# Attention of a hybrid layer: another order of rows, queries loaded by row, keys and values by separate semaphores

## The reference

```python
z = jnp.einsum('bthd,bshd->bhts', qb, kb)
strict = jnp.arange(t1)[None, :] < jnp.arange(t0, t1)[:, None]
log_beta = jax.nn.log_sigmoid(z)
log_keep = jnp.where(strict, jax.nn.log_sigmoid(-z), 0.0)
after = lax.cumsum(log_keep, axis=3, reverse=True) - log_keep
A = jnp.where(strict, jnp.exp(log_beta + after), 0.0)
outs.append(jnp.einsum('bhts,bshd->bthd', A, vb))
```

## Time and profile before

| | us |
|---|---|
| runs of the kernel, median of 3 (lowest, highest) | 3392.56 (3388.01, 3393.36) |
| the profiled execution: its own time | 3387.77 |
| the profiled execution: its span | 3386.0 |
| TensorE busy in it, matmuls | 3247.3 |
| VectorE busy in it | 2425.2 |
| ScalarE busy in it | 1926.0 |
| GpSimd busy in it | 884.7 |

### The profile page before, as it was taken

One profiled execution on the slowest core, in us unless ns is written; L12 is line 12 of the kernel. 1 busy time (PEld: TensorE's weight loads), 2 busy tenths in 40 slices (PEclk: granted clock), 3 DMA queues, 4 the chain that ended last, 5 costly groups with the idle time before them and its releaser, 6 DMA issues. The chain is left out here.

```text
span 3386.0 us, 72847 instructions
## 1 busy us (share of the span) xinstructions
PE 3247.3 (96%) x28402; PEld 2678.1 (79%) x28402; DVE 2425.2 (72%) x2989; ACT 1926.0 (57%) x4177; POOL 884.7 (26%) x677
## 2 busy tenths in 40 slices
PE   6998999999999999997999999999999998999998
PEld 4786888999999997886777677767767776888887
DVE  4765345434568894234999999989999997666665
ACT  4553112222334452224898888888889897555554
POOL 1323333200000003431223422523262325232322
PEclk8999999999999999998999999999999999999999
DMA  8889878877955578985001201120111013666664
GB/s 296 327 323 319 270 256 297 308 238 237 311 177 189 184 241 304 322 280 177 21 28 56 76 28 32 59 70 26 46 58 53 12 38 95 183 212 190 206 201 135
DMA packets 415600, 582.65 MB, mean 172 GB/s; under 512 B 35568, under 2 KB 298096, under 8 KB 414288
## 3 DMA queue, kind: packets, MB, share of 16 engines
q1 hardware_dynamic: 394560, 506.56, 45.5%
q0 software_dynamic: 16960, 58.73, 5.1%
q10 hardware_dynamic: 3792, 13.30, 1.0%
HBM read 393.74 MB, written 184.75 MB: 171 GB/s over the span
## 5 line engine op out<-in xcount | busy, mean ns | idle before, releaser
L1492 DVE TENSOR_TENSOR_SCAN a_ring<-a_ring,a_zeros 128x1024 f32<-128x1024 f32 (+6 forms) x640 | 1237.1, 2009 | 31.5 <-ACT a_ring L1417 25.6
L1431 ACT COPY a_turned<-a_rt 128x512 f32<-128x512 f32 x960 | 529.8, 622 | 113.2 <-PE a_rt L1339 112.8
L1417 ACT ACTIVATE a_ring<-a_z 128x512 f32<-128x512 f32 (+3 forms) x1152 | 561.4, 595 | 17.0 <-PE a_z L1323 16.9
L1352 PE MATMUL a_acc<-a_turned,c_dw 128*64 128x256 f32 x4352 | 524.5, 382 | 4.8 <-ACT a_osum L1441 4.8
L1339 PEld LDWEIGHTS a_rt<-c_ident,a_ring 64*128 64x128 f32 x8448 | 330.2, 138 | 179.9 <-issue 103.2
L1339 PE MATMUL a_rt<-c_ident,a_ring 64*128 64x64 f32 x8448 | 369.5, 226 | 46.4 <-ACT a_turned L1431 22.6
L1299 POOL TENSOR_SCALAR_AFFINE_SELECT a_ring<-a_ring 128x256 f32<-128x256 f32 x128 | 198.8, 1568 | 820.9 <-ACT a_ring L1417 820.9
L1352 PEld LDWEIGHTS a_acc<-a_turned,c_dw 128*64 128x64 f32 x4352 | 289.2, 137 | 152.2 <-ACT a_turned L1429 8.8
L1323 PE MATMUL a_z<-c_khi,a_q 64*128 64x512 f32 (+3 forms) x2304 | 373.2, 400 | 26.6 <-DMA c_dw<-scratch_dw 12.6
L939 DVE TENSOR_TENSOR p_hlo<-p_wraw,p_hlo 128x1024 fp32r<-128x1024 f32 x85 | 104.4, 1228 | 324.3 <-ACT p_hlo L704 324.3
L704 ACT CAST p_hlo<-p_wraw 128x1024 fp32r<-128x1024 f32 x85 | 89.1, 1048 | 392.4 <-PE p_bank L572 210.8
(11 more groups left out here) (298 smaller groups left out, 6418.9 us busy)
## 6 DMA issues: line engine op xcount, KB each, us to landing
p_hlo<-scratch_parts SPq DMA_DIRECT2D x130, 512.0 KB, 5.0
p_wraw<-scratch_sums SPq DMA_DIRECT2D x128, 512.0 KB, 6.6
p_aslot<-scratch_parts SPq DMA_DIRECT2D x62, 512.0 KB, 5.0
p_u<-in_w_in POOLq DMA_DIRECT2D x64, 256.0 KB, 5.4
scratch_wsums<-p_u POOLq DMA_DIRECT2D x32, 512.0 KB, 6.4
p_hraw<-scratch_sbv POOLq DMA_DIRECT2D x32, 512.0 KB, 7.3
m_xt<-in_x SPq DMA_DIRECT2D x32, 512.0 KB, 5.2
out_y<-c_pair SPq DMA_DIRECT2D x32, 512.0 KB, 4.5
```

Source lines behind the costliest of these rows:

```text
L1352: last = pe.matmul(acc[h * SD:(h + 1) * SD, lo:QW], dw[:, h, j * TPC + kb, :], turned[:, (FIRST[u] + kb // 2) % TB, kb % 2, h * QW + lo:(h ...
L1417: act.activation(ring[:, slot, s, part, 0:w], z[at % ZB][:, 0:w], ACT.Sigmoid, scale=-Z_SCALE).then_inc(keep_done, 1)
L1431: act.copy(dst, src).then_inc(turned_done, 1)
L1492: return dve.tensor_tensor_scan(line, line, zeros[:, 0:1].to_broadcast([P, right - left]), first, ALU.mult, ALU.add)
```

## The change

The rows of a pair of heads are taken in another order, written as a list: 15, 14, 13, 0, 12, 1, 11, 10, ... 2. The two rows of one unit so stand behind the two rows of seven units, and the last rows of a pair of heads have 2 and 2 units. Queries are loaded by row (256 columns) into four buffers; those of row r + 4 are issued when the scores of row r are all done. Keys and values of a chunk get separate semaphores: TensorE waits for the keys at the scores and for the values at the weighing. For the next heads the keys of a chunk are loaded when the scores of the last row that uses it are done, and its values behind that row's store. Row r - 1 is stored after the loads of row r. The two constants for the mixing stage move behind the last loop. Ten semaphores are passed on from the projection stage with the values that they have reached there (V_BEFORE, Q_BEFORE). The diff, cut to its core:

```diff
+    ORDER = [15, 14, 13, 0, 12, 1] + list(range(11, 1, -1))
+    FREE_AT = {}
+    for chunk in range(NCH - 1, -1, -1):
+        FREE_AT.setdefault(max(ORDER.index(2 * chunk), ORDER.index(2 * chunk + 1)) if chunk else NR - 1, []).append(chunk)
...
-        q_sb = sb("q", [P, 2, 2, CH], F32R)
+        QB = 4
+        q_sb = sb("q", [P, QB, 2, QW], F32R)
...
-        chunk_in = [sem(f"chunk_in{k}") for k in range(NCH)]
-        q_in = [sem("q_in0"), sem("q_in1")]
+        chunk_in, value_in = [sem(f"chunk_in{k}") for k in range(NCH)], loads[:NCH]
+        q_in = [sem("q_in0"), sem("q_in1"), loads[KT], loads[KT + 1]]
+        Q_BEFORE, V_BEFORE = (0, 0, 16 * NCH, 16), 32
...
                 load_keys(0, k)
+                load_values(0, k)
                 if k == NCH - 1:
-                    load_queries(sp, 1)
+                    for row in range(1, QB):
+                        load_queries(sp, row)
...
-            for g in range(NP * NCH):
-                hp, c, row = g // NCH, NCH - 1 - g % NCH, 2 * g
-                if g + 2 < NP * NCH:
-                    sp.wait_ge(z_done, 4 * (LAST[row + 1] + 1))
-                    load_queries(sp, g + 2)
...
-                store(row)
...
-                store(row + 1)
-                if hp + 1 < NP:
-                    load_keys(hp + 1, c)
-                elif c == 2:
-                    sp.wait_ge(m_out, 16)
-                    for chunk in range(2):
-                        load_mix(sp, d, mix_in, chunk, chunk, held["ch_in"])
+            def finish_row(row):
+                hp, at = row // NR, row % NR
+                store(row)
+                if hp + 1 < NP:
+                    for chunk in FREE_AT.get(at, ()):
+                        load_values(hp + 1, chunk)
+                elif at == NR - 3:
+                    sp.wait_ge(m_out, 16)
+                    for chunk in range(2):
+                        load_mix(sp, d, mix_in, chunk, chunk, held["ch_in"])
+
+            for row in range(NP * NR):
+                hp, at = row // NR, row % NR
+                sp.wait_ge(z_done, 4 * (LAST[row] + 1))
+                if row + QB < NP * NR:
+                    load_queries(sp, row + QB)
+                if hp + 1 < NP:
+                    for chunk in FREE_AT.get(at, ()):
+                        load_keys(hp + 1, chunk)
...
+                if row:
+                    finish_row(row - 1)
...
+            finish_row(NP * NR - 1)
...
-                pe.wait_ge(chunk_in[j], 64 * (hp + 1))
+                pe.wait_ge(chunk_in[j], 32 * (hp + 1))
...
             def weigh(u):
-                _, row, cb, j = UNITS[u]
+                hp, row, cb, j = UNITS[u]
+                pe.wait_ge(value_in[j], V_BEFORE + 32 * (hp + 1))
```

## The result

| | before | changed kernel |
|---|---|---|
| median of the runs, us (lowest to highest) | 3391.88 (3388.01 to 3393.36, 4 runs) | 3373.34 (3369.12 to 3377.02, 4 runs) |
| the profiled execution's own time | 3387.77 | 3377.02 |
| its span | 3386.0 | 3375.2 |

The ratio is 0.995, with a 95% interval of 0.9937 to 0.9962. The change makes the kernel 18.5 us faster on the medians; 3370 had been forecast, in a range of 3362 to 3386. The profiled execution of the changed kernel is the slowest of its four.

The account below looks back on a forecast made before the run. The vector engine's scan was taken to bound attention, so only its gaps and the end could be won. −17.06 − 5.85 + 2.1 − 2 = −22.8 us on the median 3392.56 gave 3370, range 3362 to 3386.

Parts of the forecast that it names:

- handover gaps: Scan's three gaps between pairs of heads, 5.06, 6.97 and 5.03 us, would all go with earlier queries: −17.06 us.
- mask waits: Scan of the last one-unit row waits 1.46 us for its mask, four times; the new order removes this: −5.85 us.
- gaps behind short pairs: Behind short pairs of scans the next pair waits for ScalarE's sigmoid: 7 × 0.3 = +2.1 us, bounds +1.1 to +4.0.
- length of the scans: Vector engine's scans in attention keep their total busy time: 0, with ±1.5 us for contention with gpsimd.
- separate semaphores, start of attention: First scores no longer wait for values, but first scans hang on gates and sigmoid: 0, bounds −1 to 0 us.
- end of attention, to the mixing stage's first work: After the last scan, the last store goes out sooner, mixing loads starting before that scan ends: −2 us, bounds −5 to +3.
- the seven places named: Where small sigmoid gaps were expected: behind row 12's short joined pair (four times) and row 2's before each handover (three).
- Count and elements are unchanged, so 0: Both orders have 160 scans per pair of heads with the same elements, so total scan length was put at 0 change.
- the first rival: Row 12's mask comes late as gpsimd's work slows beside the scans: 16 us given back, 3386 us; chance 8%.
- 12 to 14 us: Forecast time from attention's last scan to its last store, against 14.9 us in the kernel before.
- the third: Rival: TensorE becomes the bound, the added wait costing 0.43 us per unit instead of 0.02: 3459 us; chance 5%.
- the handover didn't stay: Denies a rival: SP held by a store issues queries no earlier, the 17.06 us stay, 3387 us; chance 4%.

Follow-up runs that it names:

- e0_after: The changed kernel run once more, nothing altered: median 3372.95 us, ratio 0.9955 to the kernel before.
- e2_late_queries: The changed kernel with the queries of the next heads' first row issued late, after the last row's last scores: 3386.72 us (1 run).
- e1_old_order: The changed kernel with the rows back in the order 15 down to 0, all else as changed: median 3366.36 us, ratio 0.9932.
- e5_early_mix: The changed kernel with the mixing stage's fourteen loads issued once row 4's scores are done, not behind its store: median 3364.09 us, ratio 0.9923.
- e3_values_with_scores: The changed kernel with the scores waiting for the values too, as when keys and values shared a semaphore: 3370.94 us (1 run).
- e4_before_four_waits: The kernel before with four added, already satisfied waits ahead of each unit's value products: 3389.82 us (1 run).

## Why the prediction was right, point by point

The forecast held on both the time and the direction: 3373.3 us against 3370, and 18.5 us of the 22.8. What carries it is the handover, three quarters of the sum, and that mechanism is shown. The rest is in part luck: the scans' length and the start, each off by about 2.6, cancel, and neither the new order nor the new end brought what it was credited with. By its steps, from the profiled executions of before and of the changed kernel:

| step | forecast | measured |
|---|---|---|
| handover gaps, mask waits, gaps behind short pairs (idle between scans) | −17.06 − 5.85 + 2.1 = −20.8 | 8.8 − 29.0 = −20.2 |
| length of the scans | 0 ± 1.5 | +2.6 |
| separate semaphores, start of attention | −1 to 0 | −2.6 |
| end of attention, to the mixing stage's first work | −2 (−5 to +3) | +2.8 (e0_after: +0.4) |
| mixing stage | none | +1.9 |
| sum | −22.8 | −15.5 (e0_after: −18.4) |

- **The handover** was right: the queries were late, the lead of seven units is enough, and the clock stayed at 1.00. e2_late_queries shows the cause. With four units of lead e1_old_order has no gap either.
- **The masks** were right by the wait (5.9 to 0) and wrong by its worth. In the changed kernel the scans grew by 2.6 us, outside the ±1.5; the pair of row 12 and row 1 is the example above. The gaps behind short pairs went to 0.8 to 1.1 us at rows 14, 12 and 10, beyond the 0.57 of the earlier trace rows; with the 0.37 of each handover the small gaps grew by 8.8 − 6.06 = 2.7, within the bounds. That is luck in part: of the seven places named, row 12 has its gap once and not four times, the gaps at rows 14 and 10 grew without being named, and those at rows 6 and 8 shrank. Against e1_old_order, where the mask waits stand, all of the 5.9 came back: the scans of the changed kernel take 1.0 us longer. The step that failed is "Count and elements are unchanged, so 0": the sum of the elements was the same, but not what lay beside them. The contention that the first rival feared came here, as longer scans and not as a late mask.
- **The end of attention** was mis-sized, and with the wrong sign. The loads were to begin 2.1 to 3.5 us ahead of the last scan's end. They began 0.76 behind it in the changed kernel and 0.9 ahead in e0_after: row 3 began to be turned 6.0 us ahead of that end, not 7.03, and the first load went out 5.1 us behind that in e0_after and 6.8 in the changed kernel, not 3.5 to 5. The difference between these two is a weighing of 3.58 us instead of 1.95 in a stretch at clock 0.67, in the changed kernel's profiled execution only. From the first load to the last store it took 16.2 to 16.9 us, not 15.9. And the forecast ended at the store: the load of the last outputs went out 7.4 us behind it, with the last of the fourteen loads and the two constants still landing, where it had been 4.2 and is 2.9 in e5_early_mix. That is the +1.9 of the mixing stage. "12 to 14 us" from the last scan to the last store was 17.6, and 15.3 in e0_after.
- **The start** was 2.6 us quicker. Against e3_values_with_scores, which makes the first scores wait for values again, 0.8 to 1.1 of it belongs to the separate semaphores, about the forecast's bound. The other 1.9 is there in every kernel with queries by row (13.6 to 14.8 against 16.6). ScalarE's first activation began 7.2 us after its first load, not 9.4. Its queries there are half as many bytes, ahead of the gate data in the same queue; that this is the reason for the 1.9 is argued, not tried.
- **The rivals**: the wait on TensorE's queue costs 0.02 us a unit (13.2 against 6.9 us in all) and nothing of the time that the runs show; e4_before_four_waits refutes the third. No mask of row 12 came late, and the handover didn't stay.

## What to carry to other kernels

Here the load that was late at one place in a loop was cured by its lead alone; reordering the work around it moved costs to other places and won nothing. Look for the lead first. Work on GpSimd that slows VectorE is put where VectorE waits anyway, or where another engine sets the pace; a wait that it seems to cause may be the cheapest place for it. Before loads are queued ahead of a barrier, add up their issue times, and if they outlast the work that is left, put them where the same queue has no store to issue.

## What the runs showed of the hardware that was not expected

Fourteen loads of 256 KB hold SP's queue for 14.0 us in e0_after and 14.8 in the changed kernel, single ones from 0.43 to 3.08. The Trainium skill (DMA: Bandwidth & Descriptors, section Issuing engines are not separate DMA queues) calls the time to initiate a DMA usually small relative to the DMA. One by one these loads agree on the whole: each landed 5.2 to 8.3 us after its issue began. But the loads overlap and their issue times add up, and here the sum set the end of a stage; moving the loads took 5.2 us off the tail. Whether SP needed that long by itself or was held back by the transfers ahead isn't shown. In the changed kernel the same load took 0.46 us to issue for the first chunk and 0.92 for the second (c_khi from scratch_m), and the DMA engines were busy for 0.56 of the time from 2836 to 2846 us and 0.75 from there to 2853.

The same waits of TensorE at the same place (0.85 and 0.78 us in the changed kernel, 0.86 and 0.78 in e0_after) were followed by a clock of 0.67 in one execution and 1.00 in the other. Windows that take in the second of these waits and the weighing behind it, the changed kernel first:

```profile
2829.60:2834.70 5.10, 4.50 (x42) 2.66 (x44) 5.10 (x4) 2.28 (x8) 0.00 (x0) 0.67 0.00 0
```

```profile
2824.20:2830.20 6.00, 3.81 (x60) 2.69 (x60) 6.00 (x5) 3.43 (x11) 0.00 (x0) 1.00 0.00 0
```

The weighing took 3.58 us in the first and 1.95 in the second. What decides between the two levels, 1.2 and 2.4 GHz, there isn't settled by these runs.
